# Who issues the stores of the transposed operands: the sync engine or ScalarE, in a bidirectional RWKV-7 encoder block

## The chip, the core and the metric

The kernel runs on one core of a Trainium2 chip. The metric is device time in microseconds (us) of one execution; smaller is better. The engines are called as in the profile: PE is TensorE (matmul), PEld its weight loads, DVE is VectorE, ACT is ScalarE, POOL is GpSimd, SP is the sync engine, which only issues transfers here. SPq and ACTq are the instruction streams of SP and ACT where they issue a transfer.

## What is computed

One encoder layer on a sequence of 1024 tokens with 1024 channels, in float32. The part that matters here is the preparation of the RWKV-7 scan:

```python
h = rms_norm(x, ln1_g);  p = h @ w_in
r, k, v, wd, ad, gd = split_cols(token_shift(p[..., :SHIFT_DIM], mu_prev, mu_next), ...)
decay = exp(-exp(w_log));  a = sigmoid(iclr_a0 + ad @ iclr_a2)
kk = normalised(k * k_k);  k = k * (1.0 + (a - 1.0) * k_a)
def step(S, inp):                      # one scan per direction z
    rt, wt, kt, vt, at, bt = inp       # at = -kk, bt = kk * a
    Sa = einsum('zbhij,zbhj->zbhi', S, at)
    S = S * wt + Sa * bt + vt * kt
    return S, einsum('zbhij,zbhj->zbhi', S, rt)
# then: group norm, bonus, gate; windowed attention beside it; output projection;
# rms_norm, gated ConvFFN (d_ff 2816), final rms_norm
```

## The kernel before

The kernel has five stages: the normalisation and the low-rank projections; a loop over four **head pairs** (`NPAIR` = 4, two heads of 64 channels on 128 partitions), which makes the operands of the chunked scan and writes them to DRAM; the projections of the attention; the scan over 32 chunks with the attention woven in; and the output projection with the ConvFFN, which is PE work almost alone. The order of each engine's work is written by hand: five instruction streams that wait for one another's semaphores. `FREE` is 1, a start value of semaphores that guard buffers.

In head pair j, PE multiplies three projections of 128 columns (keys, receptance, values: `dense`, L485), with small low-rank products between them (`whole`, L506). ACT takes the first one out of PSUM (`own_share`, L823), then runs a sigmoid (L830) on the two decay products; PE's second projection waits for the first of these sigmoids. For each direction z (0 forward, 1 backward) DVE makes `AR[z]` and `BK[z]`, PE multiplies them chunk by chunk (the gram product, L569, 128 small matmuls), and transposes `BK[z]` (L579) into two PSUM slots. ACT copies these to `BKt` (L848, L849). DVE masks the gram product into `G` (L1243). In direction 0 PE then transposes the values (L585), and ACT copies them to `vts` (L854). PE's gram product of direction 1 waits for `G` of direction 0 and for this `vts` copy, since both free the PSUM slots that it writes.

`AR[z]`, `G`, `BKt` and `vts` are stored in DRAM (`scan_d`, `v_d`). There is one `G`, one `BKt` and one `vts` for both directions and all pairs, so the next writer waits for the store. SP issues all four kinds of store, in the order AR, G, BKt (four transfers of 64 partitions with runs of 256 bytes), `vts` (two transfers, direction 0 only), and then, in direction 1, `load_gram(j, 0)`: four small loads of the gram product of direction 0 back out of `scan_d` into `M`, which DVE needs for the triangular solve (L1260, L1264) behind the pairs. SP also loads the weights of the next pair (L321). ACT's part of the pairs is a hardware loop (`Fori`), and ACT's table loads (which swap its set of functions) are placed by the compiler.

Behind the pairs, PE waits for the last `BKt` copy and for `G` (`bkt_ready`, `G_ready`) and runs six projections (`qkv`, L485). DVE solves at the same time. ACT copies each projection out and stores it (L872, L876, L880) and then stores a quarter of the solved matrices (`TI_d`, L867); SP and POOL store the rest (L385, L1083). The scan's first product (L652) waits for the loads of `TI_d` (L365).

## Time and profile before

| | |
|---|---|
| median of 3 runs | 1602.11 us |
| lowest, highest | 1599.97, 1609.76 us |
| span of the profiled execution | 1606.1 us |
| PE, DVE, ACT, POOL busy | 1478.5, 757.9, 504.4, 50.9 us |
| mean granted TensorE clock | 0.951 of full speed |
| head pairs, by the start of each pair's first projection | 49.8, 121.9, 191.7, 261.9 us; `qkv` starts at 336.1 us |

The profiled execution is one more execution, whose span from the first to the last instruction is 1606.1 us; the page gives no time around it. The table is read so: the head pairs take 286 of 1606 us, and the change is inside them. A busy time says how long an engine worked, not whether anything waited for it; the chain of waits says that.

### The profile page before, as it was taken

The page shows a single profiled execution, that of the slowest core. Times are in us where ns is not written, and L with a number is a line of the kernel's source. Part 1 is how long each engine was busy: PE and PEld are TensorE (multiplying, and loading weights), DVE is VectorE, ACT ScalarE, POOL GpSimd, SP SyncE. Part 2 cuts the span into 40 slices and gives each one's busy share as a digit, 9 for nine tenths or more (in the row PEclk, how much of TensorE's full clock was granted, in tenths as well). Part 3 has the DMA queues.
Part 4 walks back from the last instruction along what each step waited for, and adds up shares of the span by engine and source line. Part 5 has one row for each costly group of instructions (what it writes and reads, how often), then busy time and mean ns, then how long its engine had stood idle before and what let it go on. Part 6 is the DMA issues. An engine that isn't in the chain of part 4 may idle for free.

```text
span 1606.1 us, 27423 instructions
## 1 busy us (share of the span) xinstructions
PE 1478.5 (92%) x11156; PEld 1090.8 (68%) x11156; DVE 757.9 (47%) x963; ACT 504.4 (31%) x757; POOL 50.9 (3%) x47
## 2 busy tenths in 40 slices
PE   7899898989898999978978999999999999999993
PEld 3354545444577787756856888887888888788882
DVE  5665463859355567766346323321333322233345
ACT  3424142320156567664214323210222211122221
POOL 0010010101001000003000000000000000000000
PEclk9999999989879899989988999999999999999997
DMA  5036538286447475631110111111111111111112
GB/s 196 30 98 142 137 88 192 69 193 183 103 135 261 141 197 174 201 107 40 52 39 27 42 49 41 57 46 52 40 52 39 52 53 52 40 53 39 46 32 105
DMA packets 153464, 148.42 MB, mean 92 GB/s; under 512 B 75120, under 2 KB 130544, under 8 KB 153296
## 3 DMA queue, kind: packets, MB, share of 16 engines
q1 hardware_dynamic: 144976, 135.95, 29.4%
q10 hardware_dynamic: 6720, 6.29, 1.3%
q0 software_dynamic: 1728, 5.64, 1.2%
q8 instruction: 25, 0.41, 0.1%
q14 instruction: 15, 0.12, 0.0%
HBM read 106.04 MB, written 41.81 MB: 92 GB/s over the span
## 4 chain that ended last, share of the span: by engine, by line
PE 79%; DVE 9%; ACT 5%; issue 3%; DMA 2%; SPq 1%; ACTq 1%; DVEq 0%
PE banks L497 49%; PE banks L485 16%; PE banks L652 2%; PE banks L662 2%; PE banks L681 2%; PE banks L506 2%; PE banks L633 1%; ACT work L913 1%; PE banks L622 1%; PE banks L569 1%; PE banks L696 1%; DVE hT L1130 1%; PE banks L612 1%; PE banks L705 1%; DVE bonusT L1127 1%
## 5 line engine op out<-in xcount | busy, mean ns | idle before, releaser
L497 PE MATMUL banks<-h_hi,w_hi 128*128 128x512 f32 x832 | 259.9, 394 | 22.3 <-DVE h_lo L1111 17.1
L485 PE MATMUL banks<-hT,work 128*128 128x512 f32 x576 | 254.2, 601 | 19.5 <-DVE hT L1173 6.4
L497 PE MATMUL banks<-h_lo,w_hi 128*128 128x512 f32 x832 | 258.2, 392 | 0.0
L497 PE MATMUL banks<-h_hi,w_lo 128*128 128x512 f32 x832 | 257.9, 391 | 0.0
L485 PEld LDWEIGHTS banks<-hT,work 128*128 128x128 f32 x576 | 110.3, 193 | 160.4 <-issue 146.0
L497 PEld LDWEIGHTS banks<-h_hi,w_hi 128*128 128x128 f32 x832 | 156.6, 189 | 59.5 <-issue 18.2
L977 ACT ACTIVATE w_hi<-work 128x1024 fp32r<-128x1024 f32 x76 | 80.2, 1057 | 368.1 <-PE banks L497 368.1
L497 PEld LDWEIGHTS banks<-h_lo,w_hi 128*128 128x128 f32 x832 | 157.5, 189 | 33.1
L497 PEld LDWEIGHTS banks<-h_hi,w_lo 128*128 128x128 f32 x832 | 157.3, 189 | 33.2
L1395 DVE TENSOR_TENSOR xT<-xT,banks 128x1024 f32<-128x1024 f32 (+1 forms) x32 | 39.1, 1221 | 225.8 <-PE banks L497 225.8
L497 PE MATMUL banks<-g_hi,w_lo 128*128 128x512 f32 x352 | 108.4, 389 | 0.0
L497 PE MATMUL banks<-g_hi,w_hi 128*128 128x512 f32 x352 | 108.3, 389 | 0.0
L497 PE MATMUL banks<-g_lo,w_hi 128*128 128x512 f32 x352 | 108.3, 389 | 0.0
L1111 DVE TENSOR_TENSOR w_lo<-work,w_hi 128x1024 fp32r<-128x1024 f32 x76 | 93.3, 1228 | 2.0 <-ACT w_hi L977 2.0
L497 PEld LDWEIGHTS banks<-g_hi,w_hi 128*128 128x128 f32 x352 | 66.1, 188 | 13.8
L497 PEld LDWEIGHTS banks<-g_hi,w_lo 128*128 128x128 f32 x352 | 66.1, 188 | 13.7
L497 PEld LDWEIGHTS banks<-g_lo,w_hi 128*128 128x128 f32 x352 | 66.1, 188 | 13.7
L1418 DVE SCALAR_TENSOR_TENSOR sgT<-banks,par,sgT 128x1023 f32<-128x1023 f32 x11 | 14.1, 1283 | 103.6 <-ACT sgT L1020 103.6
L1418 DVE SCALAR_TENSOR_TENSOR bonusT<-banks,par,bonusT 128x1023 f32<-128x1023 f32 x11 | 14.1, 1282 | 94.4 <-ACT bonusT L1020 94.4
L1184 DVE SCALAR_TENSOR_TENSOR work<-banks,par,work 128x1023 f32<-128x1023 f32 x12 | 15.4, 1281 | 82.5 <-ACT work L823 82.5
L652 PE MATMUL banks<-work 32*64 32x64 f32 x1024 | 40.0, 232 | 11.5 <-DMA work<-v_d 4.5
L696 PEld LDWEIGHTS banks<-work 64*64 64x64 f32 x1024 | 35.8, 146 | 17.2 <-issue 17.2
(163 smaller groups left out, 1762.2 us busy)
## 6 DMA issues: line engine op xcount, KB each, us to landing
work<-scan_d SPq DMA_DIRECT2D x32, 768.0 KB, 4.8
work<-in_w_gu SPq DMA_DIRECT2D x44, 512.0 KB, 3.5
scan_d<-work SPq DMA_DIRECT2D x16, 1024.0 KB, 6.0
work<-in_w_in SPq DMA_DIRECT2D x20, 512.0 KB, 3.8
scan_d<-work SPq DMA_DIRECT2D x32, 256.0 KB, 6.2
work<-in_w_down SPq DMA_DIRECT2D x16, 512.0 KB, 3.5
work<-v_d SPq DMA_DIRECT2D x64, 64.0 KB, 4.6
y_d<-work SPq DMA_DIRECT2D x128, 32.0 KB, 2.1
```

What stands on the lines that cost most here:

```text
L485: mm = pe.matmul(out[:, h * HALF:(h + 1) * HALF], wt[:, k, :], src[:, k, h * HALF:(h + 1) * HALF], start=(k == 0), stop=(k == kn - 1))
L497: mm = pe.matmul(out[:, h * HALF:(h + 1) * HALF], wp[slot][:, k, :], xp[:, k, h * HALF:(h + 1) * HALF], start=(opens and k == (ks or range ...
L506: mm = pe.matmul(out[:, h * HALF:(h + 1) * HALF], wt, src[rows, h * HALF:(h + 1) * HALF], start=True, stop=True)
L569: mm = pe.matmul(out, BK[z][h, c].rearrange("p a b -> p (a b)"), AR[z][h, c].rearrange("p a b -> p (a b)"), start=True, stop=True)
L652: pe.matmul(XY[z][64 * e:64 * e + 64, j * HD:(j + 1) * HD], Gs[slot][hk, z, j, c2 * 64:c2 * 64 + 64], UV[slot][hk, z, c2, j, :], start=(j ...
L662: mm = pe.matmul(XY[z][h, j * HD:(j + 1) * HD], ARs[slot][h, z, j, c2 * 64:c2 * 64 + 64], S[h, z, j, :], start=False, stop=(j == NPAIR - 1 ...
L681: mm = pe.matmul(US[z][hu, j * HD:(j + 1) * HD], TIs[slot][hu, z, c2, j, :], Xs[hu, z, j * HD:(j + 1) * HD], start=True, stop=True)
L696: mm = pe.matmul(US[z][h, 256 + j * HD:256 + (j + 1) * HD], BKs[slot][h, z, j, c2 * HD:c2 * HD + HD], UV[slot][h, z, c2, j, :], start=True ...
L977: act.activation(w_hi[slot][:, :, :], w_raw[slot], ACT.Copy).then_inc(wt["hi"][slot], 1)
L1111: tt(out, x, hi.bitcast(F32), ALU.subtract).then_inc(done, 1)
L1395: tt(x, x, product, ALU.add).then_inc(added[slot], 1)
L1418: stt(g[:, 1:T], ps[2 * b][:, 0:T - 1], col("cw0", f), g[:, 1:T], ALU.mult, ALU.add)\
```

## The change

The six stores of `BKt` and `vts` of each pair leave SP's stream. ACT issues them, the four `BKt` stores directly behind the second copy into `BKt`, in front of the `vts` copy, and the two `vts` stores directly behind that copy. ACT's loop over the pairs becomes a Python loop, so its four rounds are written out one after the other. PE, DVE and POOL have the same instructions as before.

```diff
@@ SP
                     sp.wait_ge(s["G_ready"], 2 * j + z + 1 + FREE)
                     sp.dma_start(scan_d[z, :, :, 1, j, :].rearrange("c p n -> p c n"),
                                  G.rearrange("p (c q) t -> p c (q t)", q=2)).then_inc(s["G_stored"], 16)
-                    sp.wait_ge(s["bkt_ready"], 2 * j + z + 1 + FREE)
-
-                    for odd in range(2):
-                        for e in range(2):
-                            dst = scan_d[z, :, 64 * e:64 * e + 64, 2, j, HD * odd:HD * odd + HD].rearrange("c p n -> p c n")
-                            sp.dma_start(dst, BKt[64 * odd:64 * odd + 64, :, HD * e:HD * e + HD])\
-                              .then_inc(s["BK_stored"], 16)
-                    if z == 0:
-                        sp.wait_ge(s["vts_ready"], j + 1)
-                        for e in range(2):
-                            sp.dma_start(v_d.rearrange("(b p) n -> p b n", p=P)[:, :, bass.ds((e * NPAIR + j) * HD, HD)],
-                                         vts[:, :, HD * e:HD * e + HD]).then_inc(s["v_stored"], 16)
                 load_gram(j, 1)
@@ ACT
-            with act.Fori(0, NPAIR) as j:
+            for j in range(NPAIR):
...
                     act.activation(BKt[:, 8:16].rearrange("p a b -> p (a b)"), ps[0], ACT.Copy)\
                        .then_inc(s["bkt_ready"], 1)
+                    act.wait_ge(s["bkt_ready"], 2 * j + z + 1 + FREE)
+                    for odd in range(2):
+                        for e in range(2):
+                            dst = scan_d[z, :, 64 * e:64 * e + 64, 2, j, HD * odd:HD * odd + HD].rearrange("c p n -> p c n")
+                            act.dma_start(dst, BKt[64 * odd:64 * odd + 64, :, HD * e:HD * e + HD])\
+                               .then_inc(s["BK_stored"], 16)
                     if z == 0:
                         act.wait_ge(s["vt_mm"], j + 1)
                         act.wait_ge(s["v_stored"], 32 * j + FREE)
                         act.activation(vts.rearrange("p a b -> p (a b)"), ps[1], ACT.Copy).then_inc(s["vts_ready"], 1)
+                        act.wait_ge(s["vts_ready"], j + 1)
+                        for e in range(2):
+                            act.dma_start(v_d.rearrange("(b p) n -> p b n", p=P)[:, :, bass.ds((e * NPAIR + j) * HD, HD)],
+                                          vts[:, :, HD * e:HD * e + HD]).then_inc(s["v_stored"], 16)
```

In the changed file ACT's lines of the pairs have numbers lower by 12: L811 is the copy of `own_share` (L823 before), L818 the decay sigmoid (L830), L836, L837 and L848 the copies to `BKt` and `vts` (L848, L849, L854), L843 and L851 the moved stores.

On ACT, at the start of a round of the loop before:

```order
L823 ISA
L823 ACT_TABLE_LOAD
L823 ACTIVATE work<-banks,c_eps 128x1024
L829 REGISTER_ALU
L830 ISA
L830 ACT_TABLE_LOAD
L830 ACTIVATE work<-banks,par 128x32x32
```

And the same place in the second round of the changed kernel, from the last copies and stores of the first round on:

```order
L836 ACTIVATE work<-banks 128x1024
L837 ACTIVATE work<-banks 128x1024
L843 DMA scan_d<-work 64x16x64 x4
L811 ACTIVATE work<-banks,c_eps 128x1024
L818 ACT_TABLE_LOAD
L818 ACTIVATE work<-banks,par 128x32x32 x2
```

The four stores now stand between the last copy of a pair and the first copy of the next; with the loop written out, the table load in front of that first copy is gone in every round, and in the first round the one of the sigmoid is gone as well.

On ACT in the middle of a pair, before:

```order
L847 ISA
L848 ACTIVATE work<-banks 128x1024
L849 ACTIVATE work<-banks 128x1024
L854 ACTIVATE work<-banks 128x1024
```

and now:

```order
L836 ACTIVATE work<-banks 128x1024
L837 ACTIVATE work<-banks 128x1024
L843 DMA scan_d<-work 64x16x64 x4
L848 ACTIVATE work<-banks 128x1024
L851 DMA v_d<-work 128x8x64 x2
```

The `vts` copy (L854 before, L848 now) stood directly behind the `BKt` copies; now four stores are issued ahead of it.

On SP, one pair, as a difference (minus is before):

```order
 L325 DMA scan_d<-work 128x16x128
 L330 DMA scan_d<-work 128x16x128
-L337 DMA scan_d<-work 64x16x64 x4
-L342 DMA v_d<-work 128x8x64 x2
-L325 DMA scan_d<-work 128x16x128
-L311 DMA xT<-scan_d 16x32x32 x4
-L330 DMA scan_d<-work 128x16x128
-L337 DMA scan_d<-work 64x16x64 x4
+L325 DMA scan_d<-work 128x16x128
+L311 DMA xT<-scan_d 16x32x32 x4
+L330 DMA scan_d<-work 128x16x128
 L311 DMA xT<-scan_d 16x32x32 x4
```

The AR store of direction 1 (second L325) and the loads of the gram product (L311) follow the G store (L330) directly.

## Rows read from the trace of the kernel before

**Rows 1.** The page's chain that ended last: shares of the span.

```profile
PE 79%; DVE 9%; ACT 5%; issue 3%; DMA 2%; SPq 1%; ACTq 1%; DVEq 0%
```

**Rows 2.** Chain of waits, end of the second pair: start us, us, what.

```profile
179.33 1.15 DVE work L1243
...
182.52 1.03 ACT work L854
...
183.80 5.28 PE banks L569 x128
```

**Rows 3.** Chain of waits, start of the third pair.

```profile
209.51 1.12 ACT work L830
...
210.68 5.42 PE banks L485 x12
```

**Rows 4.** Timeline of ACT: start us, us, engine, line, operation, [idle before <-releaser].

```profile
178.97 1.02 ACT L849 ACTIVATE work<-banks 128x1024 f32<-128x1024 f32 x1
...
205.79 1.28 ACT L823 ACT_TABLE_LOAD   x1 [9.80 <-PE banks L485]
207.09 1.11 ACT L823 ACTIVATE work<-banks,c_eps 128x1024 f32<-128x1024 f32 x1
...
318.93 1.02 ACT L849 ACTIVATE work<-banks 128x1024 f32<-128x1024 f32 x1
321.61 1.02 ACT L854 ACTIVATE work<-banks 128x1024 f32<-128x1024 f32 x1 [1.66 <-PE banks L585]
334.11 1.02 ACT L848 ACTIVATE work<-banks 128x1024 f32<-128x1024 f32 x1 [11.48 <-DMA scan_d<-work]
...
411.39 7.37 ACTq L867 DMA_DIRECT2D TI_d<-xT  x4
```

**Rows 5.** Timeline of SP: stores of direction 0 in the second pair, and `TI_d`.

```profile
181.62 0.39 SPq L330 DMA_DIRECT2D scan_d<-work  x1
182.06 7.27 SPq L337 DMA_DIRECT2D scan_d<-work  x4
...
411.21 6.18 SPq L385 DMA_DIRECT2D TI_d<-xT  x4
```

**Rows 6.** Timeline of PE: gram products, low-rank products, transposes in pair 4 and before the scan.

```profile
171.99 3.95 PE L569 MATMUL banks<-work 64*64 64x64 f32 x128
...
183.80 5.27 PE L569 MATMUL banks<-work 64*64 64x64 f32 x128 [1.31 <-ACT work L854]
...
112.72 6.55 PE L569 MATMUL banks<-work 64*64 64x64 f32 x128 [1.31 <-ACT work L854]
...
205.60 3.81 PE L506 MATMUL banks<-work 64*128 64x512 f32 x12
...
328.31 1.97 PE L579 MATMUL banks<-ident,work 128*128 128x128 f32 x16
...
421.98 1.09 PE L598 MATMUL banks<-ident,work 128*128 128x128 f32 x8 [1.11 <-ACT work L872]
```

**Rows 7.** Engines by stretch: stretch, length, busy PE PEld DVE ACT POOL, PEclk, DMA share, GB/s.

```profile
182.00:216.00 34.00, 30.71 (x204) 17.17 (x203) 9.71 (x7) 11.99 (x11) 0.00 (x0) 0.93 0.95 205
...
184.00:186.00 2.00, 2.00 (x42) 2.00 (x42) 0.00 (x0) 0.00 (x0) 0.00 (x0) 0.50 1.03 285
...
336.00:338.00 2.00, 1.90 (x3) 0.86 (x4) 0.00 (x0) 0.05 (x1) 0.00 (x0) 0.50 1.03 290
...
424.00:460.00 36.00, 33.34 (x480) 27.07 (x482) 14.80 (x35) 9.84 (x27) 0.00 (x0) 0.53 0.33 97
```

**Rows 8.** Timeline of DVE: the first step of the solve.

```profile
341.47 0.27 DVE L1260 TENSOR_TENSOR work<-xT 128x62 f32<-128x62 f32 x1 [10.60 <-DMA xT<-scan_d]
```

**Rows 9.** Chain of waits, from `qkv` to the scan's first product.

```profile
336.10 71.04 PE banks L485 x160
...
416.54 6.27 DMA TI_d<-xT
...
426.17 1.97 PE banks L652 x32
```

## The prediction, made before the changed kernel ran

> **What bounds the kernel now.** I read the page's chain that ended last first [rows 1]. PE has 79% of it, DVE 9%, ACT 5%, and SP's stream 1%: SP is almost never what the end waits for, so taking work off SP is worth little in itself. ACT is rarely on the chain, but where it is, a delay counts in full. The next view is the chain in order of time at the end of a pair [rows 2]. There it runs from DVE's mask (L1243) through a short group of transposes to ACT's `vts` copy (182.52, 1.03 us), and from that to PE's gram product of direction 1 at 183.80. So the `vts` copy is on the path, and the change puts four stores ahead of it. The chain at the start of a pair [rows 3] shows a second place: PE's second projection (210.68) waits for ACT's first sigmoid (209.51 to 210.63), which stands behind two table loads and a copy; the first of these loads runs at 205.79, after PE has finished, so it is on the path too [rows 4].
>
> **Part 1: the four `BKt` stores ahead of the `vts` copy.** Call d the time ACT needs to issue them. In the second pair the last `BKt` copy ends at 178.97 + 1.02 = 179.99, so the `vts` copy can start at about 180.1 + d where it started at 182.52 [rows 2]: PE's gram product comes d - 2.4 later. In the fourth pair the copy ends at 319.95 and the `vts` copy began at 321.61: d - 1.6 later [rows 4]; pairs 1 and 3 look like the fourth.
>
> How large is d? On SP the four took 7.27 us [rows 5], behind a G store that has as many bytes as all four together and passed in 0.39 us because the queue was empty. So an issue is cheap until the queue is full, and then as slow as the transfers drain; the stretch is full of transfers (share 0.95 over 34 us) [rows 7]. ACT's queue is empty at this point. Lower bound: two stores at 0.39 and two at 7.27 / 4 = 1.82, 4.4 us. Upper bound: 7.27 and one more such step of 1.82 for what SP sends beside them (G at once, and now AR of direction 1 right behind it), 9.1 us. The nearest row is another place where both queues issue four small stores each at once: `TI_d` took 6.18 us on SP, whose queue was empty [rows 5], and 7.37 us on ACT, just behind four other stores [rows 4]. I take d = 6.2. Pairs 1 to 3 then lose 2 x (6.2 - 1.6) + (6.2 - 2.4) = +13.0 us (bounds +7.6 and +21.7).
>
> **Part 2: the same in the last pair.** Behind it PE does not go on at once. It waits for the last `BKt` copies, and ACT waited with these until 334.11 for the stores of direction 0 to land (11.48 us idle) [rows 4]. This hides most of the delay. With d = 6.2 the gram product, which began 0.3 us behind the `vts` copy's end (321.61 + 1.02), starts at 322.9 + 4.6 = 327.5, takes about 6.0 (5.27 and 6.55 now), the transposes 1.97 [rows 6], and the copy starts at 335.5, not 334.11: +1.4 (bounds 0, where the landing is still last, and +4.3).
>
> **Part 3: the table loads.** Writing the loop out removes the load ahead of the first copy in each of the four pairs (1.28 us, [rows 4]); in the first pair the sigmoid's goes as well. What is late next? PE's own low-rank products end at 205.60 + 3.81 = 209.41 [rows 6], against 210.68 now: the path can gain 1.27 us a pair and no more, and the second load saved in pair 1 is worth nothing. 4 x 1.27 = -5.1 us. The Trainium skill (ScalarE: Activation LUTs, "What ACT_TABLE_LOAD costs") puts a switch at 2.66 us, a drain of 1.38 us included; by it the sum would be 5.5 us lower. This trace doesn't agree: the load starts at 205.79 and the copy behind it at 207.09 [rows 4].
>
> **Part 4: stores that move past others.** The two `vts` stores on ACT and the four of direction 1 delay nobody on the path if ACT is free for the next pair's first copy. That copy waits for a projection of 14.0 us. With the numbers above the `BKt` copies of direction 1 end about 1.5 us after that projection begins, and even stores as slow as SP's 7.27 leave 5 us: cost 0, and if this cover went it would be us for us, three times. No wait is added that is not met: ACT waits for its own copies only. SP's queue is now shorter: AR of direction 1, the loads L311 and the next G store go out earlier. Only one of these has a waiter that matters, the loads of M: DVE's solve began at 341.47 after 10.60 us idle [rows 8]. But these loads lie behind the same bytes in the same 16 DMA engines, so I give the solve 1 to 2 us, not 10.
>
> **Part 5: behind the pairs.** At 336.10 PE restarted at half clock, 1.2 GHz (PEclk 0.50) [rows 7], after 5.8 us of idleness; the idle time will be about 2 us now, so the clock may hold. Worth 0 to -2 us, I take -1. From there `qkv` (71 us of the chain) leads to ACT's `TI_d` stores, their landing (6.27) and the scan's first product at 426.17 [rows 9]; PE had finished its transposes at 421.98 + 1.09 = 423.07 [rows 6], so up to 3.1 us of PE idleness lie there. Since the solve ends a little earlier and SP's share of `TI_d` starts before ACT's, I let 1.4 us be absorbed (bounds 0 and 3.1).
>
> Sum on the profiled execution of 1606.1 us: +13.0 + 1.4 - 5.1 - 1.0 - 1.4 = **+6.9 us**. That execution is 4.0 us above the median of the runs, inside their scatter (1599.97 to 1609.76), so I put the same difference on the median: 1602.1 + 6.9 = **1609**. The lower bounds together give 7.6 + 0 - 5.1 - 2 - 3.1 = -2.6, the upper ones 21.7 + 4.3 - 5.1 = +20.9. The gram product of direction 1 ran at half clock for most of its time (PEclk 0.50 at 184 to 186, [rows 7]); its 5.27 to 6.55 could be anything from 3.95 to twice that, 7.9 [rows 6], behind a longer idle time: up to 2 us a pair either way, and I take no change.
>
> **The rivals.** (A) *Faster than before: the clock at the scan's start.* From 424 to 460 us PE was busy 33.3 of 36 us at a granted clock of 0.53 [rows 7]; it fell after the idle time ahead of 426.17. If part 5 closes more of this idle time and the clock stays at 2.4 GHz, up to 0.47 x 33.3 = 15.7 us of PE time go, of which waits for ACT and DVE would take back about a third: -10. It decides once it is worth more than the sum above. For it: the gap is short and its end is a transfer that the change touches. Against: PE stays idle 1.1 us there anyway for ACT (L872), and short gaps within pairs were followed by a fall as well. Time: 1609 - 10 = 1599.
> (B) *Clearly slower: ACT's issues wait for SP's.* If only one queue can hand over transfers at a time, ACT's third and fourth store wait behind SP's G and AR stores, the latter blocked by a full queue. Then d is at its upper end, 9.1: +21.7 + 4.3 - 5.1, 1623. For it: `TI_d` on both queues took about as long on each as SP's four stores did alone. Against: these had no 1 MB store beside them, and G needs 0.39 us only. The Trainium skill (Perfetto Trace Analysis, "DMA Instruction — HWDGE (DVE, Sync)") says that the block which makes descriptors is shared and locked for one sequencer at a time, and that the wait for it counts in the issue; no row here separates the two.
> (C) *No change: ACT's empty queue takes the stores at once.* d = 4.4: 7.6 - 5.1 and the rest absorbed, +0 to +1, 1602. For it: 0.39 us for the G store. Against: the `TI_d` row of SP.
> (D) *The change doesn't do what it says*, because SP wasn't in the way: true in all cases above as far as a gain from SP is concerned.
>
> **How the numbers follow.** Forecast (+2 to +13 us) 0.45, A 0.17, B 0.20, C 0.13, others 0.05. 1% is 16 us, about what a measurement of this kernel can tell from no change. The forecast, C and nearly all of A are within it; B lies just outside, and a part of it (0.17) counts as slower. Faster by 1% needs A with C (0.05). Same: 0.78. The range takes in A, C and most of B: 1595 to 1622.
>
> **What would show it.** On ACT's timeline the four stores of direction 0 at about 6 us, and the `vts` copy behind them; on PE an idle time of about 6 us ahead of the gram product of direction 1, where 1.3 stood; no table load ahead of the copy L811, and the second projection starting as the low-rank products end; the distance from one pair's start to the next 2.5 to 3.3 us longer than in the table; `qkv` starting about 9 us later than 336.1, less idle ahead of it; SP idle between its stores. I am wrong if the four issues take 3 us or less, if PE's idle time there is hidden by something else, if the stores of direction 1 hold up the next pair's first copy, or if the granted clock in the scan differs by tens of microseconds.

## The result

| | before | changed |
|---|---|---|
| median | 1604.96 us (11 runs) | 1613.28 us (11 runs) |
| lowest, highest | 1599.97, 1609.76 us | 1605.33, 1622.16 us |
| ratio to before, 95% interval | | 1.0056 [1.0036, 1.0077] |
| span of the profiled execution | 1606.1 us | 1603.2 us |

The changed kernel is 0.56% slower, 8.3 us by the medians; the forecast was +6.9 us, 1609, with a range of 1595 to 1622. A second series of the changed kernel, told below, gave 1.0062 [1.0036, 1.0089]. Beware of the last line of the table: the profiled execution of the changed kernel is the fastest of its runs, so its span is the shorter one although its median is the longer one. Spans are therefore compared stretch by stretch here, and the sign of the result is taken from the interleaved runs alone. One of the ten runs of experiment four, below, took 2559.8 us at a granted clock of 0.589 and is left out of its ratio.

**Where PE waits in the pairs.** The view of waits, PE only, from the first projection of the pairs to `qkv`, summed over the four pairs; columns: who waited for whom, us in total, times, longest. First the kernel before:

```profile
PE banks L485 <- ACT work L849: 5.8, 1, 5.8
PE banks L569 <- ACT work L854: 5.2, 4, 1.3
PE banks L485 <- ACT work L830: 5.1, 4, 1.3
```

The same view of the changed kernel (L557, L473 are L569, L485 of before; L848, L818, L837 are L854, L830, L849 of before):

```profile
PE banks L557 <- ACT work L848: 18.6, 4, 4.8
...
PE banks L473 <- ACT work L837: 3.4, 1, 3.4
PE banks L473 <- ACT work L818: 2.2, 3, 0.7
```

The wait for the `vts` copy grew from 5.2 to 18.6 us (16.7 in the second profile of the changed kernel), the wait for the sigmoid shrank from 5.1 to 2.2, and the wait ahead of `qkv` from 5.8 to 3.4. Together that is +8.1 us, but the pairs got only 4.5 us longer (286.3 to 290.8). Most of the rest lies in PE's own work: its four gram products of direction 1 took 23.8 us before and 21.5 in this profile.

**The stores on ACT.** ACT's timeline in the second pair of the changed kernel (start us, us, engine, line, operation, idle before and releaser):

```profile
178.62 1.02 ACT L837 ACTIVATE work<-banks 128x1024 f32<-128x1024 f32 x1
179.67 4.85 ACTq L843 DMA_DIRECT2D scan_d<-work  x4
184.62 1.02 ACT L848 ACTIVATE work<-banks 128x1024 f32<-128x1024 f32 x1 [4.99 <-issue]
185.68 6.57 ACTq L851 DMA_DIRECT2D v_d<-work  x2
194.72 1.02 ACT L836 ACTIVATE work<-banks 128x1024 f32<-128x1024 f32 x1 [9.07 <-DMA scan_d<-work]
195.64 1.02 ACT L837 ACTIVATE work<-banks 128x1024 f32<-128x1024 f32 x1
196.69 8.13 ACTq L843 DMA_DIRECT2D scan_d<-work  x4
207.92 1.11 ACT L811 ACTIVATE work<-banks,c_eps 128x1024 f32<-128x1024 f32 x1 [11.27 <-PE banks L473]
209.79 1.28 ACT L818 ACT_TABLE_LOAD   x1 [0.76 <-PE banks L494]
```

The four stores take 4.85 us (5.03, 4.91 and 4.86 in the other pairs), and the `vts` copy follows at once; its idle time of 4.99 us is put down to "issue", the engine's own instructions. From the start of the last `BKt` copy to that of the `vts` copy it is 184.62 - 178.62 = 6.00 us; before it was 182.52 - 178.97 = 3.55 [rows 2, 4]. The stores of direction 1 took 8.13 us here, more than I had allowed, and still ended at 204.82, 3.1 us before PE released the next pair's first copy. No table load stands ahead of that copy. PE's timeline in the same stretch of the changed kernel:

```profile
185.90 5.30 PE L557 MATMUL banks<-work 64*64 64x64 f32 x128 [4.56 <-ACT work L848]
...
207.73 3.81 PE L494 MATMUL banks<-work 64*128 64x512 f32 x12
212.26 5.42 PE L473 MATMUL banks<-hT,work 128*128 128x512 f32 x12 [0.72 <-ACT work L818]
```

4.56 us idle ahead of the gram product where 1.31 stood [rows 6], and 0.72 ahead of the second projection where 1.27 stood [rows 3, 6].

**Behind the pairs.** The chain of waits of the changed kernel, from the last stores of direction 0 to the scan's first product (start us, us, what):

```profile
322.83 0.60 ACTq L843
...
323.47 0.69 ACTq L843
...
324.19 1.39 ACTq L843
...
325.61 12.07 DMA scan_d<-work
...
337.77 1.02 ACT work L836
...
339.76 71.99 PE banks L473 x160
...
423.15 6.20 DMA TI_d<-xT
...
433.26 1.97 PE banks L640 x32
```

The `BKt` copies of direction 1 in the last pair (L836, L837) wait for a landing of 12.07 us, and the scan begins at 433.26. The landing of `TI_d` takes 6.20 us, as before (6.27, [rows 9]). `qkv` itself took 71.99 us on the chain where it took 71.04, and the rest of the difference is mostly ACT's queue ahead of the landing. ACT's timeline there:

```profile
411.77 1.02 ACT L870 ACTIVATE work<-banks 128x1024 f32<-128x1024 f32 x1 [12.71 <-PE banks L473]
412.83 4.30 ACTq L878 DMA_DIRECT2D kk_d<-work  x4
417.17 7.41 ACTq L865 DMA_DIRECT2D TI_d<-xT  x4
```

And SP's timeline of the changed kernel, with its share of `TI_d`, which begins 1 us into ACT's `kk_d`:

```profile
413.82 5.20 SPq L373 DMA_DIRECT2D TI_d<-xT  x4
```

`kk_d` took 4.30 us; before, ACT's timeline had 3.13 for it, when SP's `TI_d` began only as it ended.

**The balance.** From PE's timelines, with each pair cut at its two gram products. The columns are sums over the pairs; "after" is the profiled execution above, "again" that of the second series.

| stretch | before | after | again |
|---|---|---|---|
| pair's start to first gram product, 4 pairs | 202.3 | 199.0 (-3.3) | 198.9 (-3.4) |
| first to second gram product, pairs 1 to 3 | 33.7 | 42.6 (+8.9) | 42.5 (+8.8) |
| the same, pair 4 | 10.9 | 14.1 (+3.2) | 14.1 (+3.2) |
| second gram product to next pair, pairs 1 to 3 | 26.2 | 24.5 (-1.7) | 27.1 (+0.9) |
| second gram product of pair 4 to `qkv` | 13.2 | 10.7 (-2.5) | 11.1 (-2.2) |
| `qkv` to the scan's first product | 90.1 | 93.5 (+3.4) | 91.7 (+1.6) |
| up to the scan's first product | 376.4 | 384.3 (+7.9) | 385.2 (+8.8) |
| the rest of the span | 1179.9 | 1169.9 | 1180.4 |

+7.9 and +8.8 us at the scan's first product agree with the +8.3 of the medians. The rest of the span, which the change doesn't touch, is 10 us shorter in one profile of the changed kernel and the same in the other. It differs from one execution to the next, in part with the granted clock (told under rival A), and it explains the short span.

### The profile page after: what moved, and what is told of

The parts are those of the page before. It is cut to its first block, busy times and chain, and to the rows that moved or that the text cites. A ratio compares the mean times of both kernels' runs of the same rounds, so it can differ in the third digit from the quotient of the medians.

```text
span 1603.2 us, 27357 instructions
## 1 busy us (share of the span) xinstructions
PE 1464.3 (91%) x11156; PEld 1080.1 (67%) x11156; DVE 757.0 (47%) x963; ACT 499.1 (31%) x752; POOL 50.9 (3%) x47
## 4 chain that ended last, share of the span: by engine, by line
PE 80%; DVE 8%; ACT 5%; DMA 3%; issue 2%; ACTq 1%; SPq 1%; DVEq 0%
PE banks L485 49%; PE banks L473 16%; PE banks L494 3%; PE banks L640 2%; PE banks L650 2%; ACT work L911 2%; PE banks L669 2%; PE banks L557 1%; DMA scan_d<-work 1%; PE banks L621 1%; PE banks L610 1%; DVE hT L1128 1%; PE banks L684 1%; DVE bonusT L1125 1%; PE banks L600 1%
## 5 line engine op out<-in xcount | busy, mean ns | idle before, releaser
L485 PE MATMUL banks<-h_hi,w_hi 128*128 128x512 f32 x832 | 259.4, 393 | 22.0 <-DVE h_lo L1109 16.8
L473 PE MATMUL banks<-hT,work 128*128 128x512 f32 x576 | 254.8, 602 | 13.4 <-DVE hT L1171 6.4
L485 PE MATMUL banks<-h_lo,w_hi 128*128 128x512 f32 x832 | 257.7, 391 | 0.0
L485 PE MATMUL banks<-h_hi,w_lo 128*128 128x512 f32 x832 | 257.5, 391 | 0.0
L473 PEld LDWEIGHTS banks<-hT,work 128*128 128x128 f32 x576 | 110.4, 193 | 154.6 <-issue 145.6
L485 PEld LDWEIGHTS banks<-h_hi,w_hi 128*128 128x128 f32 x832 | 156.4, 189 | 58.7 <-issue 17.8
L485 PEld LDWEIGHTS banks<-h_lo,w_hi 128*128 128x128 f32 x832 | 157.1, 189 | 33.0
L485 PEld LDWEIGHTS banks<-h_hi,w_lo 128*128 128x128 f32 x832 | 157.1, 189 | 32.9
L485 PE MATMUL banks<-g_hi,w_hi 128*128 128x512 f32 x352 | 108.4, 389 | 0.0
L485 PE MATMUL banks<-g_lo,w_hi 128*128 128x512 f32 x352 | 108.4, 389 | 0.0
L485 PE MATMUL banks<-g_hi,w_lo 128*128 128x512 f32 x352 | 108.3, 389 | 0.0
L485 PEld LDWEIGHTS banks<-g_hi,w_hi 128*128 128x128 f32 x352 | 66.1, 188 | 13.7
L485 PEld LDWEIGHTS banks<-g_lo,w_hi 128*128 128x128 f32 x352 | 66.1, 188 | 13.7
L485 PEld LDWEIGHTS banks<-g_hi,w_lo 128*128 128x128 f32 x352 | 66.1, 188 | 13.7
L1416 DVE SCALAR_TENSOR_TENSOR sgT<-banks,par,sgT 128x1023 f32<-128x1023 f32 x11 | 14.1, 1282 | 102.0 <-ACT sgT L1018 102.0
L1416 DVE SCALAR_TENSOR_TENSOR bonusT<-banks,par,bonusT 128x1023 f32<-128x1023 f32 x11 | 14.1, 1283 | 94.4 <-ACT bonusT L1018 94.4
L557 PE MATMUL banks<-work 64*64 64x64 f32 x1024 | 37.3, 240 | 18.6 <-ACT work L848 18.6
```

Source lines behind the costliest of these rows:

```text
L473: mm = pe.matmul(out[:, h * HALF:(h + 1) * HALF], wt[:, k, :], src[:, k, h * HALF:(h + 1) * HALF], start=(k == 0), stop=(k == kn - 1))
L485: mm = pe.matmul(out[:, h * HALF:(h + 1) * HALF], wp[slot][:, k, :], xp[:, k, h * HALF:(h + 1) * HALF], start=(opens and k == (ks or range ...
L557: mm = pe.matmul(out, BK[z][h, c].rearrange("p a b -> p (a b)"), AR[z][h, c].rearrange("p a b -> p (a b)"), start=True, stop=True)
L1416: stt(g[:, 1:T], ps[2 * b][:, 0:T - 1], col("cw0", f), g[:, 1:T], ALU.mult, ALU.add)\
```

## The experiments

Ratios are to the kernel before, run in turn with each experiment on the same chip, with 95% intervals. "Pairs" is the time from the first projection of the pairs to `qkv`, "tail" from there to the scan's first product, both from PE's timeline of one profiled execution (before: 286.3 and 90.1 us).

**One: the written-out loop alone.** The stores stay on SP.

```diff
 (kernel before, ACT)
-            with act.Fori(0, NPAIR) as j:
+            for j in range(NPAIR):
```

> The kernel before with one part of the change alone: ACT's loop over the pairs is written out, and all stores stay on SP. Theory 1 (the time goes to the issues ahead of the values' copy, and the written-out loop gives a little back): no table load ahead of the first copy; the sigmoid still has to wait for PE's first low-rank product, 1.9 us behind the end of the projection, and then (pairs 2 to 4) for its own table load, so the second projection begins 0.5 us sooner in pairs 2 to 4 and 1.2 us sooner in pair 1, -2.9 us in all, ratio to the kernel before 0.998. By the prediction's own term it would be -5.1 us, 0.997. Theory 2 (the cost is in the two queues' transfers side by side): the same -2.9, since only one queue is in use here.

Measured: 0.9948 [0.9925, 0.9971], 1594.1 us against 1605.7; pairs 281.2, tail 89.9. This half of the change is a gain by itself, larger in the runs than the expected 0.998; the repeat below gave 0.9968. PE's view of waits:

```profile
PE banks L485 <- ACT work L849: 6.2, 1, 6.2
PE banks L569 <- ACT work L854: 5.2, 4, 1.3
PE banks L485 <- ACT work L830: 2.1, 3, 0.7
```

The wait for `vts` is as before (5.2), the wait for the sigmoid has fallen to 2.1 in three pairs, and is gone in the first. Of the 5.1 us less in the pairs, 2.6 lie between a pair's start and its first gram product, where the sigmoid is, and 2.2 behind the start of the second gram product in pairs 1 to 3, of which none took 6.5 us here against two before. The second part isn't shown to come from the edit.

**Two: the `vts` copy first, then the stores.** Everything on ACT as in the changed kernel.

```diff
 (changed kernel, ACT)
+                    if z == 0:
+                        act.wait_ge(s["vt_mm"], j + 1)
+                        act.wait_ge(s["v_stored"], 32 * j + FREE)
+                        act.activation(vts.rearrange("p a b -> p (a b)"), ps[1], ACT.Copy).then_inc(s["vts_ready"], 1)
                     act.wait_ge(s["bkt_ready"], 2 * j + z + 1 + FREE)
                     for odd in range(2):
...
                     if z == 0:
-                        act.wait_ge(s["vt_mm"], j + 1)
-                        act.wait_ge(s["v_stored"], 32 * j + FREE)
-                        act.activation(vts.rearrange("p a b -> p (a b)"), ps[1], ACT.Copy).then_inc(s["vts_ready"], 1)
                         act.wait_ge(s["vts_ready"], j + 1)
```

> The changed kernel with the copy of the values (and its wait for PE's transposes) put ahead of the four BKt stores of direction 0; all stores stay on ACT. Theory 1: PE's gram product of direction 1 follows the values' copy as closely as before (1.3 us idle instead of 4.6), three pairs get 3.3 us each back, about -10 us against the changed kernel, 1603 us or ratio 0.999 to the kernel before. Theory 2: the transfers still collide, so little comes back: DVE's mask of direction 1 goes on waiting for the landing of the G store, and the ratio stays at 1.004 to 1.006.

Measured: 0.9982 [0.9957, 1.0008], 1600.7 us; pairs 285.0, tail 88.6. The wait ahead of the gram product is back at 1.31 us in every pair, so it was the four issues ahead of the copy that stood in PE's way. But the gain of experiment one isn't all there. ACT's timeline in the last pair shows why:

```profile
317.02 1.02 ACT L842 ACTIVATE work<-banks 128x1024 f32<-128x1024 f32 x1 [2.61 <-PE banks L573]
317.03 8.57 ACTq L847 DMA_DIRECT2D scan_d<-work  x4
325.63 4.93 ACTq L852 DMA_DIRECT2D v_d<-work  x2
331.92 1.02 ACT L836 ACTIVATE work<-banks 128x1024 f32<-128x1024 f32 x1 [13.87 <-DMA scan_d<-work]
```

The four stores now start when SP issues `G`, and take 8.57 us where they took 4.86 when they went out ahead of it. So they land later, the copy behind them (L836) waits 13.87 us, and PE's wait ahead of `qkv` is 8.2 us instead of 3.4. The tail is shorter for another reason: DVE's solve began at 332.71, ahead of `qkv` (333.91), SP had issued its share of `TI_d` by 405.12, and PE stood only 1.31 us idle ahead of the scan.

**Three: the hardware loop kept.** The stores on ACT as in the changed kernel, with addresses computed from the loop's register.

```diff
 (changed kernel, ACT)
-            for j in range(NPAIR):
+            with act.Fori(0, NPAIR) as j:
...
-                            dst = scan_d[z, :, 64 * e:64 * e + 64, 2, j, HD * odd:HD * odd + HD].rearrange("c p n -> p c n")
+                            dst = scan_d[z, :, 64 * e:64 * e + 64, 2, bass.ds(j, 1), HD * odd:HD * odd + HD].rearrange("c p o n -> p c (o n)")
...
-                            act.dma_start(v_d.rearrange("(b p) n -> p b n", p=P)[:, :, bass.ds((e * NPAIR + j) * HD, HD)],
+                            act.dma_start(v_d.rearrange("(b p) n -> p b n", p=P)[:, :, bass.ds(j * HD + e * NPAIR * HD, HD)],
```

> The changed kernel with ACT's hardware loop kept (the moved stores take their addresses from registers). Both theories: the table load ahead of the first copy is back, +0.5 us in pairs 2 to 4 and +1.2 in pair 1. Each of the stores has register instructions ahead of it, so the issue may take some tenths more. About +3 to +5 us against the changed kernel, ratio 1.008 to the kernel before.

Measured: 1.0101 [1.0071, 1.0131], 1620.1 us; pairs 298.0, tail 91.6. PE's view of waits has both costs:

```profile
PE banks L557 <- ACT work L848: 18.6, 4, 5.0
...
PE banks L473 <- ACT work L818: 5.1, 4, 1.3
```

18.6 us as in the changed kernel, and 5.1 us for the sigmoid as before. The other half of the change, the move of the stores, costs 1.0% when it stands alone, and the written-out loop gave about half of that back.

**Four: SP holds back the AR store of direction 1** until the four stores of direction 0 have landed. If SP's traffic made ACT's issues slow, they would get faster.

```diff
 (changed kernel, SP, behind the G store)
+                    if z == 0:
+                        sp.wait_ge(s["BK_stored"], 128 * j + 64 + FREE)
```

> The changed kernel, but SP waits for the BKt stores of direction 0 to land before it sends AR of direction 1 (as far as that store is concerned the crowd beside ACT's stores is smaller, as it was before). Theory 1: the four issues take 4.5 to 5 us still, PE's idle time ahead of the gram product stays at 4.6 us, and only the last pair gains, where the BKt stores land 3 us sooner: -2 to -3 us against the changed kernel, ratio 1.004. Theory 2: most of the loss goes, since the landing of the BKt stores falls from 12 to 7 us: ratio 1.000 or below.

Measured: 1.0041 [1.0012, 1.0070], 1611.7 us; pairs 290.1, tail 90.6. The four issues took 4.83 to 4.99 us and the distance between the two gram products stayed at 14.1 to 14.2 us: the AR store has no part in d. SP's `G` store was left where it was, so its part isn't tested here. It had one in the last landing, as the second gram product of pair 4 to `qkv` fell from 10.7 to 9.4 us. Whether the kernel gains by it is inside the intervals.

**Five: only the `BKt` stores on ACT**, the `vts` stores back on SP.

```diff
 (changed kernel, SP, behind the G store; ACT loses the same lines)
+                    if z == 0:
+                        sp.wait_ge(s["vts_ready"], j + 1)
+                        for e in range(2):
+                            sp.dma_start(v_d.rearrange("(b p) n -> p b n", p=P)[:, :, bass.ds((e * NPAIR + j) * HD, HD)],
+                                         vts[:, :, HD * e:HD * e + HD]).then_inc(s["v_stored"], 16)
```

> The changed kernel with the two stores of the values back on SP; only the four BKt stores of each direction are issued by ACT. Theory 1 (what costs is the issues ahead of the values' copy): the stores of the values lie behind that copy and cost nothing on ACT, so this is as slow as the changed kernel: 4.6 us of PE idle time ahead of the gram product of direction 1, ratio to the kernel before 1.004 to 1.006. Theory 2 (the transfers side by side): ACT's queue carries a third less in direction 0, the BKt stores land sooner, and 2 to 4 us come back, ratio 1.003.

Measured: 1.0079 [1.0054, 1.0105], 1617.7 us against 1606.8; pairs 290.8, tail 92.7. The pairs cost the same with and without the `vts` stores on ACT, so these are free there, as Part 4 of the prediction had it. The solve began 8.3 us behind `qkv`'s start instead of 4.3. The ratio is above the 1.004 to 1.006 that was expected, with an interval that overlaps those of the changed kernel.

**Six: the lateness alone.** Experiment one, with five copies on ACT in place of the four issues; no transfer moves.

```diff
 (experiment one, ACT, ahead of the wait for vt_mm)
+                        for _ in range(5):
+                            act.activation(aT, aT, ACT.Copy).then_inc(s["spun"], 1)
+                            spun[0] += 1
+                            act.wait_ge(s["spun"], spun[0])
```

> The run with the written-out loop alone (all stores on SP), and ahead of ACT's wait for the values' transposes five copies of a 128x1024 tile onto itself that nobody needs, about 5 us. No transfer is moved; ACT is just late at this one place. Theory 1: the price of the moved issues is this lateness. PE's idle time ahead of the gram product goes from 1.3 to about 5 us in all four pairs, three of them pay 3.5 to 4 us, the fourth nothing (the landing of the BKt stores hides it): +11 us against the run with the loop alone, ratio 1.002 to the kernel before. Theory 2: lateness alone costs little (0.996), and the rest is contention.

Measured: 1.0022 [1.0002, 1.0042], 1610.1 us; pairs 291.0, tail 88.8. PE's view of waits:

```profile
PE banks L569 <- ACT work L859: 19.6, 4, 4.9
...
PE banks L485 <- ACT work L831: 2.1, 3, 0.7
PE banks L485 <- ACT work L850: 2.0, 1, 2.0
```

With 19.6 us of waits for `vts` the pairs take 291.0 us, the changed kernel 290.8 and 293.5 in its two profiles. Against experiment one the delay costs +9.8 us in the pairs. So the price of the moved stores inside the pairs is their time on ACT ahead of one copy; what they do to the transfers costs nothing there that the profiles can tell. In the tail it is otherwise: 88.8 us here, 93.5 and 91.7 in the two profiles of the changed kernel. One part of this is the granted clock: over the first 10 us of `qkv` it was 1.00 here, 0.69 and 0.84 there.

**Seven: the table load as well.** Experiment one, with a sigmoid of one column behind the last copy of each pair but the fourth, so that the table is loaded while PE multiplies.

```diff
 (experiment one, ACT)
+                    if z == 1 and j + 1 < NPAIR:
+                        act.activation(warm, eps[:, 0:1], ACT.Sigmoid)
```

> The run with the written-out loop alone, and behind the last copy of pairs 1 to 3 a sigmoid of one column that nobody needs: it pulls the table load of the decay sigmoid to a time at which ACT is idle. The table load then no longer stands between the first low-rank product and the sigmoid; PE's own low-rank products are the bound, 0.7 us sooner in three pairs: -2 us against the run with the loop alone, ratio 0.993 to 0.994. If the prediction's model of this place were right (the products end 3.8 us behind the projection and nothing else is late), the loop alone would have given all of it and this run nothing.

Measured: 0.9966 [0.9946, 0.9986], 1598.9 us; pairs 279.0, tail 90.4. PE's timeline at the start of the third pair:

```profile
200.72 3.81 PE L507 MATMUL banks<-work 64*128 64x512 f32 x12
204.46 5.42 PE L486 MATMUL banks<-hT,work 128*128 128x512 f32 x12
```

The second projection now follows the low-rank products without idle time, and this stretch is 0.78 us shorter in three pairs than in experiment one (48.76 against 49.54). The profile shows 2.2 us less in the pairs than that of experiment one (1.3 less than that of its repeat, below); the runs can't tell this kernel from experiment one (0.993 to 0.994 was expected).

**Eight: a second buffer for `BKt`.** Experiment seven, with direction 1 in a buffer of its own (in the memory of `bT` and `aT`, which are free by then), so that its copies needn't wait for the stores of direction 0.

```diff
 (experiment seven)
+        BKt2 = work[:, w.at - 2 * T:w.at].rearrange("p (a b) -> p a b", b=P)
...
+                act.wait_ge(s["BK_stored"], 128 * j + FREE)
                 act.activation(aT, ps[1], ACT.Sigmoid, bias=col("a0", j)).then_inc(s["a_ready"], 1)
...
-                    act.wait_ge(s["BK_stored"], 128 * j + 64 * z + FREE)
-                    act.activation(BKt[:, 0:8].rearrange("p a b -> p (a b)"), ps[3], ACT.Copy)
+                    to = (BKt, BKt2)[z]
+                    act.activation(to[:, 0:8].rearrange("p a b -> p (a b)"), ps[3], ACT.Copy)
```

> The run before this one (early table), and a second BKt buffer for direction 1 in memory that is free at that time (bT and aT), so that ACT's copies of direction 1 no longer wait for the landing of the stores of direction 0. Both theories: nothing changes in pairs 1 to 3, where PE does not wait for these copies; in the last pair qkv begins 4 us sooner, because PE's idle time ahead of it falls from 6.2 to 2.1 us. The next pair's aT has to wait for the stores of direction 1, which should just be landed. -4 us against the run before it, ratio 0.991.

Measured: 0.9977 [0.9948, 1.0005], 1602.0 us, not the expected 0.991; pairs 276.8, tail 92.7. PE's wait ahead of `qkv` fell from 5.79 to 2.03 us, and what was won there was given back ahead of the scan:

```profile
419.77 1.97 PE L654 MATMUL banks<-work 32*64 32x64 f32 x32 [6.13 <-DMA work<-TI_d]
```

6.13 us idle where experiment one had 3.44. Counted from the start of the pairs, `qkv` comes 2.2 us sooner than in experiment seven and DVE's solve 0.7 us later (by the clock, 335.65 against 333.61), and the solve then decides when `TI_d` is stored.

**Nine: all three on top of the moved stores**, that is experiment two with the early sigmoid and the second buffer (the edits of seven and eight).

> The run with the values' copy first (all stores on ACT), plus the early table load and the second BKt buffer. With all stores on ACT the loads of M land sooner, so DVE's solve begins some 4 us sooner than with the stores on SP and is no longer what the scan waits for; and the second buffer takes the 8.2 us of idle time ahead of qkv down to 2. Start of the pairs to the scan's first product: 373.6 us in the run with the values first, less 2 (table), less 6 (buffer) gives 365, where the loop alone had 371. Ratio to the kernel before 0.990. If the moved stores were bad in themselves (contention), it would be no faster than the two buffers with the stores on SP, 0.998.

Measured: 0.9986 [0.9959, 1.0012], 1603.4 us, not the expected 0.990; pairs 283.8, tail 87.9. ACT's timeline in the last pair:

```profile
317.10 9.06 ACTq L850 DMA_DIRECT2D scan_d<-work  x4
326.19 6.20 ACTq L857 DMA_DIRECT2D v_d<-work  x2
332.44 1.02 ACT L839 ACTIVATE work<-banks 128x1024 f32<-128x1024 f32 x1 [14.33 <-issue]
```

The second buffer is worth nothing here: the copy stands behind ACT's own issues (9.06 + 6.20 us, 14.33 idle), where it waited for a landing in experiment two, and PE is idle 8.7 us ahead of `qkv`, not 2. ACT as a store engine is the bound at this place.

**Ten and eleven: repeats**, of experiment one and of the changed kernel, side by side on one chip.

> The written-out loop alone once more, on the same chip as the runs beside it. Up to the scan's first product the profile had it 5 us ahead of the kernel before, its time was 8 ahead (0.9948), and the run with the early table load, which leads up to the scan by 2 us more, had 0.9966. If what lies behind the scan's first product is the clock's luck, this comes back anywhere in 0.993 to 0.998 with the same 371 us up to the scan.

> The changed kernel once more, for a second profile on the same chip. 384 us from the pairs' start to the scan's first product and a time of 1.004 to 1.007 of the kernel before; the rest of the span is free to differ by the clock granted in the scan.

Measured: the written-out loop alone 0.9968 [0.9943, 0.9993], 1598.9 us; the changed kernel 1.0062 [1.0036, 1.0089], 1614.2 us. Pairs 280.3 and 293.5, tail 90.0 and 91.7. Both signs hold, and so do the times up to the scan's first product (370.4 and 385.2 us, expected 371 and 384). No kernel of the series beats experiment one by more than the intervals; the version to keep is the loop written out with all stores on SP, with or without the early sigmoid.

## Why the prediction held, and where it didn't

The time and the direction were right, and so was the main mechanism. That +6.9 us lies so near the measured +7.9 and +8.8 is partly luck: up to `qkv` the forecast was +9.3 us and the profiles show +4.5 and +7.2, behind it the forecast was -2.4 and they show +3.4 and +1.6. Three terms were too large in size and one had the wrong sign, and these errors nearly cancelled. The signs named for a pair and for `qkv` missed for the same reason: a pair took 1.3 to 1.7 us more in the first profile, not 2.5 to 3.3, and `qkv` began 3.7 us later, not 9.

**Part 1, d.** Predicted 6.2 us of issue time, bounds 4.4 and 9.1, and +13.0 us for pairs 1 to 3. Measured d = 4.85 to 5.03 and +8.9 us; with 4.9 in the prediction's own formula it would have been 2 x 3.3 + 2.5 = +9.1. The mechanism is shown twice: it goes when the `vts` copy is put first (experiment two), and it comes back at its full size with copies in place of the stores (experiment six). The step that was mis-sized is the row chosen for d, `TI_d` [rows 4, 5], which is issued on both queues at once; ACT's stores of direction 0 begin 1.7 us before SP's `G` (179.67 against 181.35) and are partly through by then. The reading "cheap until the queue is full, then as slow as it drains" fits the rows: on the chain of the changed kernel the first three of the four took 0.60, 0.69 and 1.39 us. No run tests it by itself. The same four stores cost 8.6 to 10.2 us when they begin with `G` or up to 0.9 us behind it (experiments two and nine), so my upper bound was a real case, of a different order.

**Part 2, the last pair.** Predicted +1.4 us, measured +3.15 - 2.52 = +0.6 (again: +1.0). Most of the delay was hidden by the wait for the last landing, as argued. But the prediction let PE's transposes be last, and it was the landing again, which had itself become late. Before, the chain there was:

```profile
327.67 6.42 DMA scan_d<-work
```

The 6.42 us here and the 12.07 of the changed kernel both count from the fourth store. From the first of the four stores (322.02 before, 322.83 now) to the end of the landing it was 12.1 us, and is 14.9 now. With experiment four holding AR back the stretch from the gram product to `qkv` was 1.3 us shorter, so the AR store is a part of it. The Trainium skill (DMA: Bandwidth & Descriptors, "Issuing engines are not separate DMA queues") says that transfers started by different engines run on the same 16 DMA engines and only the sequencer's time is saved. The rows agree: SP was freed of its stores, and they landed no sooner (14.9 us against 12.1). The sequencer's time was no small part here: 4.9 us of ACT for the four.

**Part 3, the table loads.** Predicted -5.1 us, measured -3.3 for the whole stretch in both profiles, and 5.1 to 2.2 us in the view of waits. The step that failed is "against 210.68 now: the path can gain 1.27 us a pair". It took away the load ahead of the copy and left out that the sigmoid's own load stays on the path: it starts when the first low-rank product is done (209.79, 1.28 us), not with the copy. So 0.55 us a pair in pairs 2 to 4, and the full 1.28 only in the first pair, where there is no load at all. That the second load of pair 1 "is worth nothing" was wrong for the same reason. Experiment seven, which hides that load, gets the rest. The price of one load held: in the trace of before the sigmoid's load stands right behind a copy that ended at 208.20, ran from 208.22 to 209.50, and the sigmoid began at 209.51.

**Part 4.** Right in what it costs: the stores of direction 1 and of `vts` delay nobody (experiment five). The cover was thinner than the 5 us named, 3.1 us in the worst pair: the copies waited for a landing and ended 2.9 us behind the start of the projection, not 1.5, and the issues took 8.13 us, not 7.27. The loads of M did not help: the solve began 5.4 us behind `qkv`'s start before, and 4.3 and 4.5 us behind it in the changed kernel, about 1 us sooner by that measure; but `qkv` itself was later, so by the profile's time the solve began at 344.06, not ahead of 341.47 [rows 8].

**Part 5.** The sign was wrong: -2.4 us predicted, +3.4 and +1.6 measured. The clock at `qkv`'s start was at 0.50 again, 1.2 GHz, although PE had been idle 3.4 us only and not 5.8. Over the first 10 us of `qkv` it was 0.79 before, 0.69 and 0.84 in the two profiles of the changed kernel, so the -1 became +1.0 us in one (71.99 against 71.04) and about -0.5 in the other. An idle time of 2.0 us, as the prediction had it, was followed by 1.00 in experiment six and by 0.83 in four and eight. The changed kernel by stretches (stretch, length, busy PE PEld DVE ACT POOL, PEclk, DMA share, GB/s):

```profile
340.00:342.00 2.00, 2.00 (x3) 0.93 (x4) 0.00 (x0) 0.00 (x0) 0.00 (x0) 0.50 0.98 179
...
424.00:460.00 36.00, 27.50 (x520) 21.80 (x520) 14.12 (x34) 12.47 (x30) 0.00 (x0) 0.81 0.44 123
```

The 1.4 us "absorbed" weren't there either, since the solve and `qkv` moved back nearly together, and nothing was left to absorb. What the tail was made of, in us behind `qkv`'s start, from the timelines, with the granted clock over the first 10 us of `qkv`:

| | clock | solve starts | ACT issues `kk_d` (takes) | ACT issues `TI_d` (takes) | SP issues `TI_d` | scan |
|---|---|---|---|---|---|---|
| before | 0.79 | 5.4 | 72.1 (3.1) | 75.3 (7.4) | 75.1 | 90.1 |
| one, loop only | 0.84 | 5.3 | 71.6 (3.1) | 75.0 (7.3) | 75.0 | 89.9 |
| after | 0.69 | 4.3 | 73.1 (4.3) | 77.4 (7.4) | 74.1 | 93.5 |
| again | 0.84 | 4.5 | 71.6 (3.1) | 74.7 (8.8) | 74.2 | 91.7 |
| three, loop kept | 0.84 | 4.5 | 71.6 (3.1) | 74.7 (8.5) | 74.3 | 91.6 |
| six, delay only | 1.00 | 4.6 | 70.0 (3.1) | 74.4 (6.5) | 74.3 | 88.8 |
| four, AR later | 0.83 | 7.3 | 71.7 (3.1) | 77.0 (4.6) | 77.0 | 90.6 |
| five, keys only | 0.83 | 8.3 | 71.7 (3.1) | 78.1 (5.0) | 78.1 | 92.7 |
| eight, two buffers | 0.83 | 8.6 | 71.7 (3.1) | 78.4 (5.0) | 78.4 | 92.7 |

SP's `TI_d` begins 69.7 to 69.8 us after the solve's first step in all of them. In four, five and eight the solve is late and decides: ACT's share begins with SP's. In the changed kernel ACT's own issues end last. The step of the prediction that failed is "since the solve ends a little earlier and SP's share of `TI_d` starts before ACT's": the rows show a price for it, not a gain. Compare the profiles with a clock of 0.84. In experiment one both shares begin together and ACT's takes 7.3 us. In "again" and in three the solve is 0.8 us sooner, SP's share begins while ACT still issues `kk_d`, ACT's share then takes 8.5 to 8.8 us, and the scan begins 1.7 to 1.8 us later. In "after" the lower clock put `kk_d` later still, SP's `TI_d` began 1 us into it, and it took 1.2 us more. In experiment six the solve is as early, but with the clock at 1.00 `kk_d` was through 1.2 us before either share began, and ACT's took 6.5 us. This is read from single profiles and no experiment moves it alone, so the cause is argued and not shown.

**The rivals.** *A, the clock at the scan's start*, did not decide, but its price is real in single executions. The window from 424 to 460 us holds 9 us ahead of the scan in the changed kernel. Over the 36 us behind the scan's first product the clock was 0.79 in the changed kernel and 0.66 in the repeat, where before had 0.53. The rest of the span was 10.0 us shorter with 0.79, the very size that A named, and 0.5 us longer with 0.66. PE had been idle longer ahead of the scan, 5.6 and 5.3 us against 3.1, so my reason, a shorter idle time, is refuted, and the changed kernel's runs are slower all the same. In the thirteen profiles the four with the shortest rest (1169.9 to 1172.2 us) had 0.78 to 0.83 there and the three with the longest (1182.4 to 1185.4) 0.57 to 0.67, but two more with 0.78 and 0.83 stand at 1176.9 and 1180.2: the clock there is a part of the scatter and not all of it. *B, d at 9.1*, didn't happen in the changed kernel and did in experiments two and nine, where the copy that PE waits for stood ahead of the stores; whether there a lock or the full DMA engines held ACT's issues isn't told apart by any run. *C, d = 4.4*, was nearer in d than my value, but missed the rest of the sum. *D* is right in its content: SP wasn't in the way, and freeing it bought nothing in the changed kernel.

## What to carry to other kernels

A store issued by a compute engine costs that engine the issue time, and the price is paid by whatever stands behind it in its stream: here 4.9 us ahead of one copy that PE waits for, four times. Before moving stores, look for the first instruction behind them that someone waits for, and put that one first; and measure the parts of an edit apart, since the gain here came from a side effect (a loop written out) and the intended part lost two to three times as much (1.0% against 0.3 to 0.5%). When a wait is shortened, follow the chain once more from the engine that is released to the operation that it needs, table load included: of an expected 1.27 us a pair only 0.55 was to be had in three of the four pairs.

## What the hardware showed that I had not expected

- Four stores of 64 partitions on an empty ACT queue took 4.85 to 5.03 us to issue when they began 1.7 us ahead of SP's 1 MB `G` store, and 8.6 to 10.2 us when they began with it or up to 0.9 us behind it. On SP, behind `G` in one queue, they took 7.27 [rows 5].
- The gram product of direction 1, the same 128 matmuls, took 5.2 to 6.0 us in most pairs and 6.4 to 6.7 in some: in two of four pairs before and in experiment three, where the loop is kept, and in one of four or none in the eleven profiles with the loop written out. It didn't follow the idle time ahead of it (5.3 us behind 1.31 as behind 4.9). I had left it open by 2 us a pair; the cause stays open.
- The rest of the span, behind the scan's first product, differed from 1169.9 to 1185.4 us between profiles of kernels that are the same there, more than the whole effect of the change.
